# Fourier mix of a transformer block: the same transform with half the channel and half the token frequencies

## The reference

```python
def fourier_mix(f):
    fg = f.reshape(B, N, 4, 128)
    y = jnp.fft.fft2(fg, axes=(1, 3), norm="ortho").real
    return y.reshape(B, N, 512)

def merge_branches(f_mix, att, gates, w_fourier, w_mla_o, b_gate, w_out):
    g = jax.nn.sigmoid(gates + b_gate)
    g_f, g_a = g[..., :D_MODEL], g[..., D_MODEL:]
    y = g_f * (f_mix @ w_fourier) + g_a * (att @ w_mla_o)
    return y @ w_out
```

## Time and profile before

| | us |
|---|---|
| median of three runs (3283.58 to 3285.79) | 3284.54 |
| the profiled execution | 3285.72 |
| its span, first to last instruction | 3283.9 |
| PE busy | 3062.3 |
| DVE, ACT, POOL busy | 1503.3, 919.1, 1084.3 |
| mean granted clock of PE | 0.977 |

### The profile page before, as it was taken

One profiled execution on the slowest core, in us unless ns is written; L12 is line 12 of the kernel. 1 busy time (PEld: TensorE's weight loads), 2 busy tenths in 40 slices (PEclk: granted clock), 3 DMA queues, 4 the chain that ended last, 5 costly groups with the idle time before them and its releaser, 6 DMA issues.

```text
span 3283.9 us, 38081 instructions
## 1 busy us (share of the span) xinstructions
PE 3062.3 (93%) x15219; PEld 2546.2 (78%) x15219; DVE 1503.3 (46%) x2253; ACT 919.1 (28%) x1598; POOL 1084.3 (33%) x482
## 2 busy tenths in 40 slices
PE   6999998999989799999999999999899999989996
PEld 2888876888768688888888777888687877877785
DVE  4843113888544431313132344445526566664555
ACT  4122212666201210101010111321325455553412
POOL 1333265000134844444343344234232121121242
PEclk8999999999999999999999999999899999999998
DMA  5534544232141411111111121111141111211112
GB/s 220 180 109 144 186 131 128 68 83 54 71 153 51 148 52 52 45 51 45 51 45 51 45 64 52 46 39 52 34 167 53 58 52 52 58 52 46 33 52 83
DMA packets 113886, 258.93 MB, mean 79 GB/s; under 512 B 46640, under 2 KB 64512, under 8 KB 109776
## 3 DMA queue, kind: packets, MB, share of 16 engines
q1 hardware_dynamic: 113744, 256.95, 23.9%
HBM read 214.54 MB, written 42.38 MB: 78 GB/s over the span
## 4 chain that ended last, share of the span: by engine, by line
PE 66%; issue 17%; DVE 8%; ACT 4%; POOL 4%; DMA 1%; SPq 0%; POOLq 0%; ACTq 0%; DVEq 0%
PE ps L363 20%; PE ps L364 20%; PE ps L365 20%; ACT tmp L1508 2%; POOL whi L705 2%; PE ps L1405 2%; DVE tmp L2585 2%; POOL wlo L707 2%; PE ps L1391 1%; PE ps L803 1%; DVE Z L1982 1%; DVE mx L2369 1%; DVE ETb_lo L1979 1%; DVE acc L1982 0%; PE ps L983 0%
## 5 line engine op out<-in xcount | busy, mean ns | idle before, releaser
L705 POOL TENSOR_TENSOR whi<-raw,onesf 128x1024 fp32r<-128x1024 f32 x235 | 456.8, 1944 | 2116.8 <-PE ps L365 2055.2
L707 POOL TENSOR_TENSOR wlo<-raw,whi 128x1024 fp32r<-128x1024 f32 x235 | 615.7, 2620 | 18.4
L363 PE MATMUL ps<-Hb_hi,whi 128*128 128x512 f32 x1424 | 573.8, 403 | 13.0 <-DVE Y L2342 5.9
L365 PE MATMUL ps<-Hb_hi,wlo 128*128 128x512 f32 x1424 | 556.6, 391 | 0.0
L364 PE MATMUL ps<-Hb_lo,whi 128*128 128x512 f32 x1424 | 556.0, 390 | 0.0
L363 PEld LDWEIGHTS ps<-Hb_hi,whi 128*128 128x128 f32 x1424 | 268.8, 189 | 64.2 <-issue 13.0
L365 PEld LDWEIGHTS ps<-Hb_hi,wlo 128*128 128x128 f32 x1424 | 267.9, 188 | 58.0
L364 PEld LDWEIGHTS ps<-Hb_lo,whi 128*128 128x128 f32 x1424 | 268.9, 189 | 47.8
L1508 ACT ACTIVATE tmp<-tmp,mx 128x1280 f32<-128x1280 f32 (+2 forms) x192 | 187.1, 974 | 108.6 <-DVE mx L2585 90.9
L1508 ACT ACTIVATE tmp<-ps 64x256 f32<-64x256 f32 (+1 forms) x96 | 57.2, 596 | 554.0 <-PE ps L365 480.9
L363 PE MATMUL ps<-Uhi,whi 128*128 128x512 f32 x512 | 199.2, 389 | 0.0
(11 more groups left out here) (408 smaller groups left out, 5952.9 us busy)
## 6 DMA issues: line engine op xcount, KB each, us to landing
raw<-in_w SPq DMA_DIRECT2D x221, 512.0 KB, 3.4
adas<-in_ada SPq DMA_DIRECT2D x16, 1024.0 KB, 4.8
raw<-in_w SPq DMA_DIRECT2D x36, 256.0 KB, 3.9
adaE<-in_ada SPq DMA_DIRECT2D x4, 2048.0 KB, 23.6
gate_d<-gst SPq DMA_DIRECT2D x16, 512.0 KB, 2.6
v_d<-VS SPq DMA_DIRECT2D x2, 4096.0 KB, 15.4
ncB<-cum_d SPq DMA_DIRECT2D x16, 512.0 KB, 3.7
Vx<-v_d SPq DMA_DIRECT2D x16, 512.0 KB, 4.5
```

What stands on the lines that cost most here:

```text
L363: nc.tensor.matmul(o, wh, xh, start=start, stop=False)
L365: return nc.tensor.matmul(o, wl, xh, start=False, stop=stop)
L705: nc.gpsimd.tensor_tensor(whi[b][:, 0:w], raw[b][:, 0:w], onesf[:, 0:1].to_broadcast([P, w]), ALU.mult).then_inc(S("split_hi"), 1)
L707: nc.gpsimd.tensor_tensor(wlo[b][:, 0:w], raw[b][:, 0:w], f32(whi[b][:, 0:w]), ALU.subtract).then_inc(S("split"), 1)
```

## The change

1. The sums over channels come first (`channels`, P): for each of 8 token tiles and 4 groups, 3 matmuls with the tile as the weight and 128 columns of D: 65 cosines, 63 sines. P is packed: 64 cosines of each group, then the 65th and the sines.
2. The sums over tokens follow for frequencies 0 to 511 only: four panels of cosines (`cosines`, C, 22 matmuls) and four of sines (`sines`, S, 12). Frequency 512 comes from a one-row product with alternating signs, turned to columns by three transposes.
3. `f` is computed with channels on partitions.
4. The Fourier weights of the merge are folded (row u with row 128 - u: sum Wa, difference Wm). For this SP copies 63 rows in DRAM during `gates`, four per tile, then loads Wa and Wb, DVE adds and subtracts, SP stores the result in DRAM, and the merge panels take half their columns from there. Channel frequency 64 goes through a 96-row product (W64, E64).
5. In the merge the two Fourier products go to the two halves of a pair. DVE adds them for tokens 0 to 511 and subtracts them in reverse order for tokens 1023 to 513; token 512 comes from two-column products. `dft` goes from 20 panels to 8; the merge loops are unrolled.

```diff
+DFT_ORDER = (("P", 0), ("P", 1), ("P", 2), ("P", 3), ("C", 0), ("P", 4), ("P", 5), ("S", 0), ("P", 6), ("P", 7),
+             ("C", 1), ("S", 1), ("C", 2), ("S", 2), ("C", 3), ("S", 3))
+P_BANK = (4, 5, 6, 7, 0, 1, 0, 1)
...
                 for t in range(16):
                     store_gate(t)
+                    for u in range(4 * t, 4 * t + 4):
+                        if u:
+                            turned_row(u)
...
             if on("dft"):
-                for h in range(2):
-                    for j in range(10):
-                        load_panel("dft", 10, h, j)
-                    if h == 0 and on("mla"):
...
+                sp.wait_ge(S("wf_moved"), ROWS64)
+                sp.wait_ge(S("panel_done"), P0["dft"])
+                for s_ in range(2):
...
+                    for b in range(2):
+                        g = 2 * b + s_
+                        sp.dma_start(Wa[r, :, b, :], fourier[:, 0:NOPE, P * g:P * g + P].rearrange("t u c -> u t c")).then_inc(S("wf_moved"), 16)
+                        sp.dma_start(Wb[NOPE * s_ + 1:NOPE * s_ + NOPE, :, b, :], wr_d[1:NOPE, :, g]).then_inc(S("wf_moved"), 16)
...
+                if on("mla"):
+                    for x in range(2):
+                        head_qk(x)
+                        head_rates(x)
+                for j in range(8):
+                    if j == 4:
+                        sp.wait_ge(S("dft_lo"), made_low("wp"))
+                        sp.dma_start(wf_d[:, :, 0:2, :].rearrange("t p b c -> p t b c"), Wa[:, :, :, :]).then_inc(S("wf_moved"), 16)
+                        sp.dma_start(wf_d[:, :, 2:4, :].rearrange("t p b c -> p t b c"), Wm[:, :, :, :]).then_inc(S("wf_moved"), 16)
+                        sp.wait_ge(S("wf_moved"), ROWS64 + 16 * 15)
+                    load_panel("dft", 8, 0, j)
...
+                def cosines(n):
+                    wh, wl = panel("dft", 8, 0, 2 * n)
+                    pe.wait_ge(S("dft_lo"), made_low(f"p{max(2 * n + 1, 3)}"))
+                    for m in range(3):
+                        o = ps[:, (4 + m) * HALF:(5 + m) * HALF] if m < 2 else ps[0:4, 6 * HALF:7 * HALF]
+                        c = slice(P * m, P * m + P) if m < 2 else slice(256, FW, 64)
...
+                    for k in range(2):
+                        for x in (Phi, Plo):
+                            kt = 2 * n + k
+                            last = nc.tensor.matmul(ps[0:1, 7 * HALF:8 * HALF], Dhi[:, P:P + 1], x[:, kt, :], start=kt == 0 and x is Phi, stop=kt == 7 and x is Plo)
+                    done(last)
...
             if on("mla"):
-                act.wait_ge(S("fm_lo"), 8 + PRIMED["fm_lo"])
+                act.wait_ge(S("wf_moved"), ROWS64 + 16 * 15)
...
             if on("merge"):
                 act.wait_ge(S("ml_at"), 8)
...
+                for t in range(9):
+                    if t < 8:
+                        act.wait_ge(S("dft_s"), t + 10)
+                        if t >= 2:
+                            act.wait_ge(S("y_full"), t - 1)
+                        copy(p2c[t % 2][:, :], pair_of("merge", 2 * t)[0][:, HALF:T], S("dft_hi"))
+                    if t:
+                        act.wait_ge(S("y_full"), t)
+                        copy(Yhi[:, t - 1, :], mm1[:, :], S("y_hi"))
...
+                for t in range(8):
...
+                    nc.vector.tensor_reduce(mm1[:, HALF:HALF + 1], ps[:, c:c + 2], AXX, ALU.add).then_inc(S("dft_lo"), 1)
+                    dve.wait_ge(S("dft_hi"), made_high(f"f{t}"))
+                    tt(mm1[:, 0:HALF], f[:, 0:HALF], p2c[t % 2][:, :], ALU.add, S("dft_lo"))
+                    tt(mm1[:, T - 1:HALF:-1], f[:, 1:HALF], p2c[t % 2][:, 1:HALF], ALU.subtract, free)
+                    dve.wait_ge(S(f"sg_loaded{t % 2}"), 32 * (t // 2) + 32)
...
+                    tt(mm1[:, :], mm1[:, :], sg[t % 2][0], ALU.mult, S("dft_lo"))
+                    panels_done(dve, "merge", 8, 0, t)
+                    g, free = pair_of("merge", 2 * t + 1)
+                    tt(mm2[:, :], g, sg[t % 2][1], ALU.mult, free)
...
+                    tt(mm1[:, :], mm1[:, :], mm2[:, :], ALU.add, S("y_full"))
+                    dve.wait_ge(S("y_hi"), t + 1)
+                    sub(Ylo[:, t, :], mm1[:, :], Yhi[:, t, :], S("y_lo"))
```

More of the change, by code:

```diff
@@ L45 @@
 NCOLS = _n
-PANELS = (("lat", 4), ("f", 4), ("gates", 20), ("dft", 20), ("merge", 8), ("wout", 8),
+PANELS = (("lat", 4), ("f", 4), ("gates", 20), ("dft", 8), ("merge", 8), ("wout", 8),
           ("mem", 16), ("mlp", 64), ("pool", 21), ("mem1", 7), ("out1", 12), ("foxv", 4), ("forget", 1), ("foxw", 4), ("fox", 25), ("mem2", 7), ("out2", 12))
@@ L54 @@
     _n += _w
-STREAM_GAP = 13
+STREAM_GAP = 25
 NP = _n + STREAM_GAP
@@ L402, in placed @@
             def placed(buf, q):
+                if P0["dft"] <= q < P0["merge"]:
+                    n = q - P0["dft"]
+                    return [(buf[:, :], d["w"][DFT_AT + n // 2 + (4 if WAVES[n] == "S" else 0)])]
+                if P0["merge"] <= q < P0["wout"]:
+                    t = q - P0["merge"]
+                    return [(buf[:, 0:HALF], wf_d[t].rearrange("p b c -> p (b c)")),
+                            (buf[:, HALF:PW], d["w"][16 + STREAM_GAP + q][:, HALF:PW])]
                 p0 = P0["gates"]
@@ L556, in sp_program @@
             if on("mla"):
-                sp.wait_ge(S("panel_done"), P0["dft"] + 20)
+                sp.wait_ge(S("dft_s"), 8)
                 head_v(0)
@@ L693, in twice @@
             def twice(n):
-                two = [P0["gates"] + 2, P0["gates"] + 3] + [P0["fox"] + kq_panel(h) for h in range(FOX)]
+                two = [P0["gates"] + 2, P0["gates"] + 3] + list(range(P0["merge"], P0["wout"])) + [P0["fox"] + kq_panel(h) for h in range(FOX)]
                 return sum(1 for m in two if m <= n and (m - n) % 2 == 0)
@@ L739, in pool_program @@
             if on("dft"):
-                with gp.Fori(0, 2) as i:
-                    splits("dft", 10, 10, i)
-            for stage, per, n in (("merge", 2, 4), ("wout", 2, 4), ("mem", 8, 2), ("mlp", 16, 4)):
+                splits("dft", 0, 8)
+            if on("merge"):
+                splits("merge", 0, 8)
+            for stage, per, n in (("wout", 2, 4), ("mem", 8, 2), ("mlp", 16, 4)):
                 if on(stage):
@@ new lines, in pe_program @@
+                pe.wait_ge(S("dft_hi"), made_high("d"))
+                pe.wait_ge(S("dft_lo"), made_low("d"))
+                for kind, n in DFT_ORDER:
+                    {"P": channels, "C": cosines, "S": sines}[kind](n)
+                pe.wait_ge(S("dft_hi"), made_high("row"))
+                for b in range(2):
+                    nc.tensor.transpose(ps[:, 7 * HALF + b:7 * HALF + b + 1], row[:, P * b:P * b + P], ident[0:1, 0:1])
+                nc.tensor.transpose(ps[0:4, 7 * HALF + 2:7 * HALF + 3], row[:, 256:FW:64], ident[0:1, 0:1]).then_inc(S("dft_s"), 1)
@@ L1041, in scores @@
                             pe.wait_ge(S("ml_inv"), 3 * h)
+                        if c0 == T and not t:
+                            pe.wait_ge(S("dft_lo"), made_low("y10"))
                         if c0 == T and t:
@@ L1697, in act_program @@
                 act.wait_ge(S("ml_at"), 8)
-                with act.Fori(0, 4) as i:
-                    for j in range(2):
-                        act.wait_ge(S("y_full"), 2 * i + j + 1)
-                        copy(Yhi[:, 2 * i + j, :], mm1[:, :], S("y_hi"))
+                for t in range(9):
[7 more added lines that the diff above has]
+                        copy(Yhi[:, t - 1, :], mm1[:, :], S("y_hi"))
             if on("wout"):
@@ new lines, in dve_program @@
+                tt(flat(Wa), flat(Wa), flat(Wb), ALU.add, S("dft_lo"))
+                for b in range(2):
+                    dve.wait_ge(S("dft_hi"), made_high(f"y1{b}"))
+                    sub(Y1[1][:, b, :], ps[:, (4 + b) * HALF:(5 + b) * HALF], Y1[0][:, b, :], S("dft_lo"))
+                dve.wait_ge(S("dft_hi"), made_high("e1"))
+                sub(E64[64:68, 0:HALF], ps[0:4, 6 * HALF:7 * HALF], E64[0:4, 0:HALF], S("dft_lo"))
+                for b in range(2):
+                    dve.wait_ge(S("dft_hi"), made_high(f"y2{b}"))
+                    sub(Y2[1][:, b, :], ps[:, (2 + b) * HALF:(3 + b) * HALF], Y2[0][:, b, :], S("dft_lo"))
```

228 lines of the change are left out of this document (150 added, 78 removed).

## The result

The changed kernel takes 3234.57 us (median of four runs, 3226.32 to 3238.89), the kernel before on the same chip 3284.06 (3282.47 to 3285.79). The ratio is 0.985, 95% interval 0.983 to 0.986: less than 2%, but clear of the noise, a gain of 49.5 us and not of 81.5. The time lies 6.6 us above the upper end of the range and within 3 us of what rival B gave.

A forecast was written before the change was run, and what follows sets the result against it. The prediction took TensorE, with 66% of the chain, to bound the kernel. Savings of 60.4 us in the Fourier stage and 21.1 in the merge summed to 81.5, giving 3203 us, range 3184 to 3228.

The forecast's parts named there:

- rival B: Transfers dearer: weights 31 instead of 7.8 us (+23), gate tiles caught behind wlo (+6), 3232 us; chance 0.22 with what lies between.
- just enough cover: Start of attention: head 0's values land at 503, TensorE takes them at 505.0; two us of cover, beyond it each us costs one.
- The write in reverse: Merge, DVE: between the 0.68 us of forwards and twice that, at most 4.8 us in all; 0.68 taken.
- rival D: Gates' stage: a row transfer from memory to memory occupies SP for its whole flight; 3299 us, slower; chance 0.03.
- Weights: 2.0 MB at 256 GB/s = 7.8 us: Fourier stage: time for the weight transfers queued ahead of dft panel 4, which was to land at 465.3.
- upper end of 31 us: Fourier stage: the weights' time if each of the eight large transfers took 3.9 us from issue to landing.
- with a second load command ahead of it and the semaphore 10.9: Merge: the gate tiles land 10.9 us after the end of the attention part (A) of the tile before.
- 9.85: Merge cycle per tile in us: POOL's whi 1.9, products f and g 1.2 each, hand-overs 0.1, attention part A 5.44.
- rival C: One-column row at 0.82 (+5), merge stays at 12.5 per tile by DVE's and POOL's turns (+21), fold late by 10: 3239; chance 0.04.
- one us later: Merge: gates landing one us later fall into wlo's turn, giving a cycle of 12.3 us and 93 us in all.
- rest only shifts: All stages other than Fourier and merge keep their work and only shift; later stages 2320.7 us before and in the forecast.
- The rows' cost in the gates' stage: Four row transfers go out per gate tile ahead of the panel's load; 1.4 us on the path, at tile 0.

## Why the prediction was wrong

**Right.** The direction, and the mechanism in the Fourier stage: PE is no longer what ends last; panel 4 waits behind what SP issues ahead of it; the clock is 0.50 when C2 starts; P, C, S and the one-column row cost what was said (C0 starts after 1.50 us of waiting; the row's matmuls 0.23 apart). The values had just enough cover: first value matmul at 516.26 without a wait, issued at 509.35. The write in reverse costs what a forward one does, as the group of DVE's instructions with both forms shows (ns min/median/max). A transfer from memory to memory takes SP 606/607/1277 ns, so rival D was far off.

```profile
L2112 DVE TENSOR_TENSOR mm<-ps,p2c x16: 680/680/692, 810.9 to 893.0; 128x512 f32<-128x512 f32 x8, 128x511 f32<-128x511 f32 x8
```

**Wrong, first: the price of the weights.** The step "Weights: 2.0 MB at 256 GB/s = 7.8 us" should have read 20. Panel 4 came 12.5 us late: SP started 1.5 us later than reckoned, the weights took 12.1 us more (19.9), the heads and the panel 1.0 less (21.7 for 22.7). I took the rate of the heads' transfers and stayed near the fast end because a panel in short pieces takes 3.9 us to land and not 3.4. That compares single transfers with the DMAs free; it measures latency. Here eight are queued together, and windows of the changed kernel show 138 to 157 GB/s from 438 to 450. The Fourier stage became 11.8 us longer than forecast, and half the bytes gave 8 to 11 back. My upper end of 31 us had the value well inside; the choice between the ends was wrong, and rival B, with 0.22, described the case in this part. That its total, 3232, came within 3 us is luck in good part: it had 23 us here where 12 came, 6 in the merge where 12 came, and nothing for the later stages. By the Trainium skill (DMA: Bandwidth & Descriptors, section "Why small descriptors are slow (HBM only)") each piece carries a fixed cost besides its bytes, so that small pieces lose bandwidth. The rate in the windows agrees, 140 against 229 GB/s, but the panel behind them came no earlier with 4 KB pieces than in other executions with 512 bytes, so by these runs the bytes queued ahead decide. Why 1 MB less gives 8 to 11 us and a faster rate for the same bytes nothing clear, these runs don't settle; the heads' transfers behind the 4 KB pieces ran slower.

**Wrong, second: the gate tiles.** The step "with a second load command ahead of it and the semaphore 10.9" took the landing from a tile of the kernel before. In the changed kernel the product starts 13 us after A of the tile before: SP issues the two gate tiles at 822.31, for 0.90 us, behind two panel loads, which await a split that POOL ends 5.3 us after A instead of 4.4, because DVE's add got in between its two halves (wlo 3.25 us). The rows, from POOL's, SP's and DVE's timelines:

```profile
818.19 3.25 POOL L775 TENSOR_TENSOR wlo<-raw,whi 128x1024 fp32r<-128x1024 f32 x1
...
822.31 0.90 SPq L646 DMA_DIRECT2D sg<-gate_d  x2
...
829.18 1.41 DVE L2112 TENSOR_TENSOR mm<-mm,sg 128x1024 f32<-128x1024 f32 x1 [5.20 <-DMA sg<-gate_d]
```

The cycle then isn't 9.85 for each tile but 14.4 and 8.7 in turn. Their mean, 12.0, is what the prediction had named as the sign of rival C, but the cause isn't C's turns of DVE and POOL. The late one also drops the clock: PE idles 3.4 to 3.7 us three times, and the stage runs at 0.91. In the prediction "one us later" was the end of the range, 93; it was two us and the clock. With the gates in time the stage took 79.6 us, below the forecast too. The turn of DVE and POOL that I had built the cycle on never set it: with the gates in time all eight products f take 1.23 us and PE is the bound at 9.0. Where both do meet, the trace shows the price, 2.66 instead of 1.23 us for the same product at 874.47.

**Wrong, third: "rest only shifts".** Stages with the same code lost 6.7 us (2 to 8 in the nine executions), 4.2 of them in stalls that come from the place of a loop in TensorE's program. The sum had put this term at nothing, with no row for it. No view of the kernel before could show this; an allowance was in order, since the change moves everything behind it.

**Smaller.** The rows' cost in the gates' stage, said to be 1.4 at tile 0. Over ten profiled executions with the rows in the change's place, matched with the kernel before, tile 0 costs between -0.1 and 1.8 us, and tile 7 another 0.7 to 5.3: there the panels come late, POOL's splits take up to 3.37 instead of 1.9 to 2.4 us and PE's gap grows from 1.54 to 5.87 us. In sum 2.3 to 6.1 us. The programs are the same up to there, so this varies between executions, and is part of the spread of 12 us that the changed kernel shows.

## What to carry to other kernels

A stage that gets shorter moves every transfer into denser traffic and leaves each less time to land. So recompute the arrival of all that is loaded late (gate tiles here), not only of what the change adds, and price added transfers by the windows of a moment with as many in flight, not by the landing time of a single one. When one wait is taken away, write down the next two with their room: here came, one behind the other, the panel, the values, and the stores, and only the order that served all three brought the gain. And where the edit is large, expect a few us in code that it does not touch, and compare the number of instruction transfers on the two pages.

## What the runs showed of the hardware

- Three stalls of 0.3 to 1.2 us in one large loop, without a releaser, that depend on how many matmuls stand ahead of the loop in TensorE's program: there with 0 and 64 more, gone with 12 and 28 more. With them go 31 instruction transfers of 16 KB in the loop, without them 6.
- The same 2 MB: 138 to 157 GB/s in pieces of 512 bytes (windows from 438 to 450), 229 in pieces of 4 KB (442 to 446); SP's command takes 0.64 to 2.4 us with the one and 0.5 with the other.
- Evicting 511 elements in reverse order takes the same 0.68 us as 512 forwards.
